# GpSimd's long instructions in pieces, and GpSimd makes the low halves of the feed-forward weights in the sample stage

## The reference

```python
mod = silu(c) @ w_ada + b_ada                    # six vectors per row group: sh1, sc1, g1, sh2, sc2, g2
h   = rmsnorm(x, g_norm1) * (1 + sc1) + sh1
proj = h @ w_in                                   # split for HGRN2 (4 heads), Mamba-2 SSD (8), RWKV-7 (4)
mix = concat(o_hgrn2, y_ssd, o_rwkv7) @ w_out     # each from its own recurrence and gate
x   = x + g1 * mix
h   = rmsnorm(x, g_norm2) * (1 + sc2) + sh2
ff  = (silu(h @ w_gate) * (h @ w_up)) @ w_down    # inner width 2816
y   = rmsnorm(x + g2 * ff, g_final)
```

## Time and profile before

| what | value |
|---|---|
| median of three | 1761.56 us |
| the profiled execution: its own time | 1766.11 us |
| its span | 1764.4 us |
| busy in all: WLO on VectorE, line 2488 | 249.7 us, 237 times |
| busy in all: WHI on ACT, line 2002 | 266.4 us, 294 times |
| busy in all: WLO on GpSimd, line 1137 | 122.9 us, 57 times |
| TensorE, lines 1392 to 1394 with HAH/HAL | 275.9, 273.2 and 272.7 us, 832 each |

### The profile page before, as it was taken

One profiled execution on the slowest core, in us unless ns is written; L12 is line 12 of the kernel. 1 busy time (PEld: TensorE's weight loads), 2 busy tenths in 40 slices (PEclk: granted clock), 3 DMA queues, 4 the chain that ended last, 5 costly groups with the idle time before them and its releaser, 6 DMA issues.

```text
span 1764.4 us, 32641 instructions
## 1 busy us (share of the span) xinstructions
PE 1586.9 (90%) x13639; PEld 1448.9 (82%) x13639; DVE 1056.0 (60%) x2154; ACT 659.9 (37%) x1133; POOL 247.0 (14%) x329
## 2 busy tenths in 40 slices
PE   4799999979999687788897999998799999999997
PEld 2698888768888454667787999987799999999997
DVE  5513456777664577887874354865655565655554
ACT  2323333223333434434433443343443444533333
POOL 4421111111010210432244201000000000000000
PEclk9899999888999679788898999999999999999998
DMA  8111001111111366121133534543455544554552
GB/s 325 42 48 48 25 25 31 41 41 34 49 55 36 106 235 201 58 81 46 37 89 114 161 108 124 153 146 103 121 173 159 154 123 136 159 172 132 149 148 75
DMA packets 276683, 188.09 MB, mean 107 GB/s; under 512 B 7879, under 2 KB 264376, under 8 KB 275512
## 3 DMA queue, kind: packets, MB, share of 16 engines
q1 hardware_dynamic: 266050, 160.28, 30.4%
q0 software_dynamic: 7536, 22.47, 3.7%
q10 hardware_dynamic: 2950, 3.24, 0.5%
HBM read 172.82 MB, written 13.18 MB: 105 GB/s over the span
## 4 chain that ended last, share of the span: by engine, by line
PE 69%; DVE 19%; ACT 5%; issue 4%; DMA 2%; SPq 0%; POOL 0%; DVEq 0%; ACTq 0%; POOLq 0%
PE bank L1392 16%; PE bank L1393 16%; PE bank L1394 16%; PE bank L1326 3%; PE bank L1414 3%; PE bank L1415 2%; PE bank L1416 2%; ACT WHI L2002 1%; DVE WLO L2488 1%; PE bank L1423 1%; PE bank L1558 1%; PE bank L1566 1%; DVE HD L3023 1%; PE bank L1568 1%; PE bank L1797 1%
## 5 line engine op out<-in xcount | busy, mean ns | idle before, releaser
L2488 DVE TENSOR_TENSOR WLO<-RAW,WHI 128x1024 fp32r<-128x1024 f32 (+4 forms) x237 | 249.7, 1054 | 266.6 <-ACT WHI L2002 265.4
L2002 ACT CAST WHI<-RAW 128x1024 fp32r<-128x1024 f32 (+4 forms) x294 | 266.4, 910 | 179.5 <-PE bank L1394 160.6
L1392 PE MATMUL bank<-HAH,WHI 128*128 128x384 f32 (+1 forms) x832 | 275.9, 332 | 13.6 <-DVE HAL L2605 4.2
L1393 PE MATMUL bank<-HAL,WHI 128*128 128x384 f32 (+1 forms) x832 | 273.2, 328 | 0.0
L1394 PE MATMUL bank<-HAH,WLO 128*128 128x384 f32 (+1 forms) x832 | 272.7, 328 | 0.0
L1392 PE MATMUL bank<-MIXR,WHI 128*128 128x384 f32 (+2 forms) x528 | 174.0, 330 | 15.1 <-DVE WLO L2488 6.6
L1137 POOL TENSOR_TENSOR WLO<-RAW,WHI 128x1024 fp32r<-128x1024 f32 (+1 forms) x57 | 122.9, 2158 | 416.5 <-ACT WHI L2002 416.5
L1392 PEld LDWEIGHTS bank<-HAH,WHI 128*128 128x128 f32 x832 | 159.4, 192 | 19.0 <-issue 13.4
L1393 PE MATMUL bank<-MIXR,WHI 128*128 128x384 f32 (+2 forms) x528 | 170.4, 323 | 0.0
L1394 PE MATMUL bank<-MIXR,WLO 128*128 128x384 f32 (+2 forms) x528 | 170.3, 323 | 0.0
L1393 PEld LDWEIGHTS bank<-HAL,WHI 128*128 128x128 f32 x832 | 159.4, 192 | 0.1
(11 more groups left out here) (582 smaller groups left out, 3040.8 us busy)
## 6 DMA issues: line engine op xcount, KB each, us to landing
RAW<-in_w_gate SPq DMA_DIRECT2D x66, 512.0 KB, 3.9
RAW<-in_w_up SPq DMA_DIRECT2D x66, 512.0 KB, 3.9
RAW<-in_w_ada SPq DMA_DIRECT2D x32, 512.0 KB, 4.7
RAW<-in_w_in SPq DMA_DIRECT2D x26, 512.0 KB, 3.9
RAW<-in_w_out SPq DMA_DIRECT2D x24, 512.0 KB, 3.6
RAW<-in_w_down SPq DMA_DIRECT2D x32, 384.0 KB, 3.2
RAW<-in_w_down SPq DMA_DIRECT2D x32, 320.0 KB, 2.9
ADAW<-in_w_ada SPq DMA_DIRECT2D x8, 1024.0 KB, 20.4
```

What stands on the lines that cost most here:

```text
L1392: mm(bank[:, 0:w], whi[:, k, :], hi_k, start=(k == 0), stop=False)
L1393: mm(bank[:, 0:w], whi[:, k, :], lo_k, start=False, stop=False)
L2002: a.copy(w_split(i)[0][:, 0:nk, :], RAW[u % NRAW][:, 0:nk, :]).then_inc(w_hi, 1)
L2488: v.tensor_tensor(wlo[:, 0:nk, :], RAW[u % NRAW][:, 0:nk, :], whi[:, 0:nk, :].bitcast(F32), ALU.subtract).then_inc(w_lo, 1)
```

## The change

A low half on GpSimd is made in pieces of at most two blocks (256 elements) and no longer in one instruction; XDE and CE are made in two instructions each. Only the last piece counts up the semaphore. And `LO_BY` gives GpSimd the splits up to the item `sm9` of PLAN2: 92 more than before (52 of 1024 elements, 16 of 512, 16 of 384, 8 of 768). VectorE makes the remaining 136.

```diff
-                LO_BY[arg] = 'pool' if at < samples_at else 'dve'
+                LO_BY[arg] = 'pool' if at < PLAN2.index(('sm9', 0)) else 'dve'
...
-                g.tensor_tensor(wlo[:, 0:nk, :], RAW[u % NRAW][:, 0:nk, :], whi[:, 0:nk, :].bitcast(F32),
-                                ALU.subtract).then_inc(w_lo, 1)
+                for k in range(0, nk, 2):
+                    r = slice(k, min(k + 2, nk))
+                    last = g.tensor_tensor(wlo[:, r, :], RAW[u % NRAW][:, r, :], whi[:, r, :].bitcast(F32), ALU.subtract)
+                last.then_inc(w_lo, 1)
...
-                g.tensor_tensor(XDE[:, :, :], XD[:, :, :], ES[:, b, :].unsqueeze(2).broadcast_to([P, 8, 64]),
-                                ALU.mult).then_inc(mb_pool, 1)
+                for h in (0, 4):
+                    last = g.tensor_tensor(XDE[:, h:h + 4, :], XD[:, h:h + 4, :],
+                                           ES[:, b, h:h + 4].unsqueeze(2).broadcast_to([P, 4, 64]), ALU.mult)
+                last.then_inc(mb_pool, 1)
                 pool.wait_ge(mbf_act, step(MBF_ACT, 'E2', b))
-                g.tensor_tensor(CE[:, :, :], E2[:, :, :], XB[5][:, b * BLK:(b + 1) * BLK].unsqueeze(1).broadcast_to([P, 4, P]),
-                                ALU.mult).then_inc(mb_pool, 1)
+                for h in (0, 2):
+                    last = g.tensor_tensor(CE[:, h:h + 2, :], E2[:, h:h + 2, :],
+                                           XB[5][:, b * BLK:(b + 1) * BLK].unsqueeze(1).broadcast_to([P, 2, P]), ALU.mult)
+                last.then_inc(mb_pool, 1)
```

## The result

Over 16 executions each the changed kernel has a median of 1774.45 us (1762.41 to 1785.17), the kernel before 1766.10 (1754.03 to 1772.63). The ratio is 1.0054, 95% interval 1.0037 to 1.007: slower by half a per cent, where 0.8% faster was forecast.

A forecast was written before the change was run, and what follows sets the result against it. TensorE, busy 90% of the span, was taken as the bound, so VectorE or GpSimd changes pay only where it idles. 6 + 9 + 0 = 15 us: 1766.1 to 1751, or 1747 by the median; range 1731 to 1772.

The forecast's parts named there:

- part 2: Sample stage: moving 92 low halves to GpSimd gains 11, loses 7 and 2: +2 us (-20 to +18), counted as nothing.
- the steady units of 1024: Sample stage: nothing lost; TensorE takes 4.2 or 3.5 us each, GpSimd 3.0, and both halves fit behind two units.
- Part 1: GpSimd pieces of 256 elements shorten VectorE's blocking: 6 us gained from 130 to 590 us, 9 from 720 to 985.
- The 6 us for 130 to 590 us: RWKV steps: 15 VectorE instructions stretched about 22 us; pieces were to gain 6 us (between 0 and 11).
- the sentence on the next piece: 130 to 590 us: after one piece the next two-input VectorE instruction meets the next piece, so 6 us, not 9.6.
- the prediction's own sign of being wrong: Wrong if 985 to 1310 us gets longer by over 8 us, or 720 to 985 us does not get shorter.
- the SSA wait: At 1241 us: TensorE's 4.5 us wait shrinks as VectorE's queue empties, then held by the next low half: 2 us gained.
- the ring of VectorE and ACT: Down units of 384 elements from 1204 us: VectorE and ACT wait in turn, 2.08 us a unit; the move gains 3 us.
- The waits forecast at the first unit and at 1021 us: Sample stage, high half late on ACT: GpSimd's low half adds 1.75 us at 1021 us, the same at 986.
- A: Rival, slower: GpSimd bounds the sample stage between 1225 and 1277 us; 10 to 18 us lost, 1768 us; chance 0.18.
- B: Rival, no change: pieces cut up the blocking without removing it; part 1 gives 2 us, part 2 nothing: 1760; chance 0.25.
- C: Rival, more: lock and lateness go, TensorE's clock rises from 0.86 in 720 to 985 us; 29 us, 1733; chance 0.15.

The follow-up runs named there:

- e4: Pieces everywhere, only the 40 short low halves of the sample stage moved to GpSimd, against the kernel before: ratio 0.9975, sample stage 322.7 us.
- e6: Pieces everywhere, the 40 short and the 28 long low halves of 384-column units moved, against the kernel before: ratio 1.0070, sample stage 338.6 us.
- e1: Pieces only (low halves, XDE and CE), no low halves moved, against the kernel before: ratio 0.9966, block stage 259.1 us, sample stage 323.4 us.

## Why the prediction was wrong

**The step that failed** is the sentence of part 2 that in the steady units of 1024 nothing is lost, since "a unit's high and low half (4.2 us) fit behind the two units ahead of it". That reckoned from when ACT could begin the high half by the slots. ACT begins it later, behind the SGF of its own queue and the sample steps that wait for TensorE (6.7 us at unit 73, 4.6 ahead of unit 86). The runs showed in its place that moving the 28 long low halves of 384-column units costs 15.9 us of the stage (e4 to e6), and that TensorE's idle time ahead of them goes from 2.0 us to 12.1. Among these units the prediction had priced only the first (1.75 us), the changes from short down units (0.5 to 0.9 us each) and the DMA issues (2 us in all).

The trace before had a warning. A unit's slack is the time from the end of its low half to the moment when TensorE's matmul counter says that it came to the unit. Of the 52 long low halves VectorE ended 10 after that moment, 11 less than 1.6 us ahead, and 31 more than that. What the 21 lack to 1.6 us, each late one counted as 1.6, adds up to 22.5 us, so the sign could have been had. Unit 73 is one of the 11 (slack 0.98 us; after, short by 0.64), so are 86, 88, 90 and 121 (1.35, 0.96, 1.00 and 0.39; after -0.24, -1.91, -0.93 and -1.70), and 104 was near (1.80; after -2.66).

But the sum has neither the size nor the place. 7.1 of the 22.5 us lie at the 28 units, which lost 15.9, and 15.4 at the other 24, which lost nothing in balance. At 143 and 145, two of the 24, VectorE had been late because of its own queue (it began 4.1 and 3.6 us behind the high half), and the move took these waits away (1.1 and 0.9 us, after 0.2 and none). At 104, 121 and 88 the added time was more than 1.6 us, since the low half was held or stood behind DMA issues. And 4.2 us of the stage are TensorE's longer busy time at the lower granted clock. How the 15.9 us divide between plain length, holding, the queue and the clock stays open.

**Part 1.** The mechanism was right: VectorE waits for one piece and then goes in between. A low half of 1024 takes 2.8 us in four pieces without a clash, estimated 3.0 (bounds 2.4 and 3.4); SSA beside it 0.77 us, forecast 0.9 to 1.3. The block stage gives 6 us in e1 and up to 10.7 over all kernels with that code, forecast 9. Part of that is clock: for the same 2104 matmuls TensorE is busy 3.0 us less in e1 (221.9 us, granted clock 0.87) and 8.2 us less in the changed kernel. The 6 us for 130 to 590 us did not come, as far as can be told: VectorE's stretching goes only from 21 us in 12 instructions to 16 in 37, as the sentence on the next piece feared, and the ratio of e1 leaves little for it beside the block stage. Part 1 in all: 6 us measured (interval 3 to 9), 15 forecast.

**Part 2.** Forecast 0 us (sum +2, between -20 and +18), measured 15.5 us of loss in the stage (338.9 against e1's 323.4). It was the prediction's own sign of being wrong: a stage longer by over 8 us. The waits for GpSimd's low halves, forecast at some 10 us, are 31.7. Some gains came about where said: the SSA wait went from 4.5 to 1.8 us, and from unit 129 to 136, where the ring of VectorE and ACT stood, TensorE takes 14.0 us for 16.0 (forecast 3 us). But from unit 77 to 85, down units of 512, it takes 20.2 for 18.7, so that e4, with all the short ones moved, is only 0.7 us below e1. The waits forecast at the first unit and at 1021 us came too: TensorE's pause at unit 66 went from 0.55 to 3.02 us, at unit 74 from 2.16 to 3.37. Behind the DMA issues of sr4 the low half of unit 88 begins 1.0 us after its high half is ready, and TensorE waits 2.06:

```profile
1063.63 0.51 POOL L1242 DMA_DIRECT2D mb_bc<-STOKEN  x1
1064.15 3.80 POOL L1139 TENSOR_TENSOR WLO<-RAW,WHI 128x256 fp32r<-128x256 f32 x5
...
1067.41 0.66 PE L1398 MATMUL bank<-HAH,WHI 128*128 128x384 f32 x1 [2.06 <-POOL WLO L1139]
```

At sr6 they are the reason that a gain failed: the low half of unit 99, late on VectorE by 3.7 us, begins 2.7 us late on GpSimd, behind four DMA issues. I had counted this wait among the gains.

The clock had no term in part 2. The granted clock fell from 0.98 to 0.97, and TensorE's busy time for the same 1785 matmuls rose by 4.2 of the 14.4 us; the other 10.3 are idle time.

**The rivals.** A had the right sign, nearly the right size (1768 given, 1771 by ratio) and the wrong place: it put the loss between 1225 and 1277 us, with GpSimd and the lock as the bound. GpSimd is busy 40.7 of 54 us there, and the stretch got shorter. The loss sits in the wider units before it, with no engine as the bound: a latency that had less slack than was thought. That A's time came out so near is luck. B was right about 130 to 590 us, as far as can be told. Of C one sign came, and in the place that it named: the granted clock from 720 to 985 us is 0.89, before 0.86, and TensorE's busy time in the block stage is 8.2 us less. Its 1733 us did not.

## What to carry to other kernels

Work handed to a slower engine costs not where its consumer waits today but wherever the slack is less than the added length; take each instance's slack from the trace (the consumer's arrival less the producer's end) and add up what is lacking, before saying that a steady state hides it. Here that sum gave the sign and not the place: leave out the instances that are late only because of the engine that is being relieved, and add what the new engine's queue and its shared access will put on top. A queue's order sets when the input comes, so slack reckoned from buffers alone is too kind. Cutting a long GpSimd instruction where VectorE's two-input instructions stand on the path was worth having here by itself; two edits with opposite signs are worth timing apart.

## What the runs showed of the hardware

GpSimd's pieces, one right behind the other, hardly overlap: pieces of 128, 256 and 512 elements take 0.46, 0.74 and 1.30 us (medians), and four of 256 back to back 2.81 us, where one instruction of 1024 takes 2.39. So a cut costs about 0.14 us here, not the 0.2 of the fixed part. A VectorE instruction held by a piece runs before the next piece, even where four stand ready in GpSimd's queue: the longest of the 14 SSA sums between 740 and 800 us in the kernels with pieces of 256 and 128 elements took 0.89 us. The other way round a low half of four pieces took up to 5.3 us beside VectorE's two-input instructions (unit 110), for 2.81 undisturbed.
